# RWKV chunk solve: the second merge level computed on its 64x64 quarter, and independent products moved between the merge steps

## The reference, cut to what matters

```python
def step(S, inp):
    r_t, w_t, k_t, v_t, a_t, b_t = inp
    sa = jnp.einsum('bhvk,bhk->bhv', S, a_t)
    S = (S * w_t[:, :, None, :] + sa[..., None] * b_t[:, :, None, :]
         + v_t[..., None] * k_t[:, :, None, :])
    return S, jnp.einsum('bhvk,bhk->bhv', S, r_t)
```

## Time and profile before

| | us |
|---|---|
| median of 3 runs (lowest to highest) | 2050.32 (2049.99 to 2055.86) |
| the profiled execution: its own time | 2051.84 |
| the profiled execution: span | 2049.4 |
| TensorE busy in the span | 1933.6 |
| VectorE / ScalarE / GpSimd busy | 1138.7 / 761.1 / 693.6 |

### The profile page before, as it was taken

How to read it: one execution, slowest core, us unless ns; L and a number is a source line. 1 busy time by engine, 2 the same in 40 slices (tenths; PEclk the granted TensorE clock), 3 DMA queues, 4 the chain that set the end, 5 groups by cost and what they waited for, 6 DMA issues and landing times. The chain is left out here.

```text
span 2049.4 us, 26280 instructions
## 1 busy us (share of the span) xinstructions
PE 1933.6 (94%) x10768; PEld 1565.2 (76%) x10768; DVE 1138.7 (56%) x1425; ACT 761.1 (37%) x1121; POOL 693.6 (34%) x391
## 2 busy tenths in 40 slices
PE   8998999999999899999999999989989898999994
PEld 6777889998888777788998888869868784555552
DVE  5258755556765427766555676442135335666664
ACT  3345210333222343511132322343346645555552
POOL 0458210324444246821142444434410012333330
PEclk8999999999999999999999999989979998999997
DMA  7322300214444332220021554434310067999973
GB/s 312 95 89 75 103 1 1 84 62 154 176 175 154 118 98 84 81 83 1 21 83 62 194 175 156 137 115 159 113 32 2 21 257 275 343 346 357 344 286 132
DMA packets 78143, 284.63 MB, mean 139 GB/s; under 512 B 27284, under 2 KB 27412, under 8 KB 60741
## 3 DMA queue, kind: packets, MB, share of 16 engines
q1 hardware_dynamic: 71140, 272.36, 38.0%
q0 software_dynamic: 6144, 8.40, 1.2%
q10 hardware_dynamic: 736, 2.14, 0.3%
HBM read 274.44 MB, written 23.63 MB: 145 GB/s over the span
## 5 line engine op out<-in xcount | busy, mean ns | idle before, releaser
L1474 POOL TENSOR_TENSOR wmem_r<-wmem,wmem_r 128x1024 fp32r<-128x1024 f32 x170 | 420.4, 2474 | 665.7 <-ACT wmem_r L998 654.7
L681 PE MATMUL banks<-h_hi_r,wmem_r 128*128 128x512 f32 x1632 | 512.8, 394 | 13.5 <-POOL wmem_r L1474 7.7
L681 PEld LDWEIGHTS banks<-h_hi_r,wmem_r 128*128 128x128 f32 x1632 | 309.0, 189 | 82.0 <-POOL wmem_r L1474 9.5
L998 ACT ACTIVATE wmem_r<-wmem 128x1024 fp32r<-128x1024 f32 x170 | 180.2, 1060 | 484.7 <-DMA wmem<-wstream 481.7
L681 PE MATMUL banks<-hT_r,wmem_r 128*128 128x512 f32 x816 | 319.7, 392 | 0.0
L681 PEld LDWEIGHTS banks<-hT_r,wmem_r 128*128 128x128 f32 x816 | 154.7, 190 | 32.4 <-issue 0.5
L2042 PE MATMUL banks<-wmem_r,gm_mem_r 128*80 128x512 f32 x496 | 178.2, 420 | 0.0
L2570 POOL TENSOR_TENSOR wmem_r<-wmem,wmem_r 128x1024 fp32r<-128x1024 f32 x30 | 74.8, 2492 | 235.4 <-ACT wmem_r L2110 235.4
L1714 POOL DMA_INDIRECT y_tok_dram<-ztp,y_idx x32 | 66.4, 2075 | 221.3 <-DVE ztp L2496 214.8
L702 PE MATMUL banks<-wmem_r,h_hi_r 128*128 128x256 f32 x768 | 140.4, 285 | 0.0
L1414 DVE SCALAR_TENSOR_TENSOR ztp<-xT,c_act,ztp 128x256 f32<-128x256 f32 x168 | 126.6, 754 | 6.0
(11 more groups left out here) (422 smaller groups left out, 3358.0 us busy)
## 6 DMA issues: line engine op xcount, KB each, us to landing
wmem<-wstream SPq DMA_DIRECT2D x206, 512.0 KB, 3.6
slots<-experts SPq DMA_DIRECT2D x80, 1024.0 KB, 6.6
xT<-ada SPq DMA_DIRECT2D x24, 1024.0 KB, 5.8
xT<-experts SPq DMA_DIRECT2D x16, 1024.0 KB
slots<-ada SPq DMA_DIRECT2D x8, 1024.0 KB, 17.8
x_keep<-xT SPq DMA_DIRECT2D x2, 2048.0 KB, 17.6
xT<-x_keep SPq DMA_DIRECT2D x2, 2048.0 KB, 9.2
dil_rows<-dil_once SPq DMA_DIRECT2D x1, 2560.0 KB
```

The costliest lines, as they stand in the source:

```text
L681: mm = nc.tensor.matmul(o, r(lhs[:, k, :]), r(rhs[:, k, :]), start=(k == 0 and i == 0), stop=(k == KD - 1 and i == 2))
L998: inc(nc.scalar.activation(r(chunk(b)[0]), w, ACT.Copy), "w_high")
L1474: inc(g.tensor_tensor(r(lo), lo, r(hi), ALU.subtract), "w_split")
```

## The change

It has three parts. (1) At the second level the mask leaves one 64x64 quarter, so p is computed on it alone: contracted rows 0 to 63, weight columns 64 to 127, moving columns 0 to 63, output partitions 64 to 127. VectorE copies it (no mask) into the unused quarter of `tt`, called `corner`. zn is then another 64x64x64 product, rows 64 to 127 to output partitions 0 to 63, added to the quarter of Z. Four heads of a group now fill 256 columns of a bank on 64 partitions. (2) Products that need no merge result are issued elsewhere on TensorE: w's state products between the two p groups of level 1, w's value products after them, y's state products between p and zn of level 2, y's value products after zn. The u products wait for Z in two groups. (3) The job list follows the new order of opening banks, and since w and y are opened earlier than they are full, the counts that drains wait for come from a table FULL. The mask constant has 128 columns in place of 256.

The core of the diff (the rest passes FULL[name] where JOB[name] + 1 stood, and cuts the constant):

```diff
             for l in range(NL):
                 for g in range(2):
+                    if (l, g) == (0, 1):
+                        job(f"w{n}", "w_ready", 1 + n)
                     job(f"p{n}{l}{g}", "p_ready", 1 + 2 * NL * n + 2 * l + g)
+                if l == NL - 1:
+                    job(f"y{n}", "y_ready", 1 + n)
                 for g in range(2):
...
-            job(f"w{n}", "w_ready", 1 + n)
             job(f"u{n}", "u_ready", 1 + n)
-            job(f"y{n}", "y_ready", 1 + n)
...
+        FULL = {name: j + 1 for name, j in JOB.items()}
+        for n in range(NT):
+            for late, sooner in ((f"w{n}", (f"p{n}01",)), (f"y{n}", (f"zn{n}{NL - 1}0", f"zn{n}{NL - 1}1", f"u{n}"))):
+                FULL[late] += len(sooner)
+                for name in sooner:
+                    FULL[name] -= 1
...
+                def state_part(o, z):
+
+                    for c in range(CW):
+                        nc.tensor.matmul(o[:, c * P:c * P + P], z[:, c, t0:t0 + P], state[:, c, :],
+                                         start=(c == 0), stop=False, skip_group_check=True)
+
+                def value_part(o, k, last):
+
+                    for h in range(RW_H):
+                        cols = slice(h * 64, h * 64 + 64)
+                        mm = nc.tensor.matmul(o[:, cols], gm[:, h, k, :], v_tok[:, n, cols],
+                                              start=(n == 0 and h == 0), stop=(last and h == RW_H - 1), skip_group_check=True)
+                    return mm
+
+                for g in range(2):
+                    if g == 1:
+                        o_w = open_bank(f"w{n}")
+                        if n > 0:
+                            after("s_ready", n)
+                            state_part(o_w, KK)
+                    after("gram_ready", 8 * n + 4 * g + 4)
+                    after("tinit_ready", 2 * n + 1 + g)
+                    o = open_bank(f"p{n}0{g}")
+                    for i in range(4):
+                        u = 4 * g + i
+                        mm = nc.tensor.matmul(o[:, i * P:i * P + P], gm[:, u, 0, :], tt[:, u, :], start=True, stop=True)
+                    full(mm)
                 if n == 0:
                     after("tok_ready")
...
+                full(value_part(o_w, 2, True))
...
+                for g in range(2):
+                    after("t_ready", 2 * (NL - 1) * n + 1 + g)
+                    o = open_bank(f"p{n}1{g}")
+                    for i in range(4):
+                        u = 4 * g + i
+                        mm = nc.tensor.matmul(o[LOWER, i * HALF:i * HALF + HALF], gm[UPPER, u, 0, LOWER], tt[UPPER, u, UPPER],
+                                              start=True, stop=True)
+                    full(mm)
+                o_y = open_bank(f"y{n}")
                 if n > 0:
...
+                    state_part(o_y, R_)
+                for g in range(2):
+                    after("p_ready", 2 * NL * n + 3 + g)
+                    after("z_ready", 2 * NL * n + 1 + g)
+                    o = open_bank(f"zn{n}1{g}")
+                    for i in range(4):
+                        u = 4 * g + i
+                        mm = nc.tensor.matmul(o[UPPER, i * HALF:i * HALF + HALF], corner[LOWER, u, UPPER], zt[LOWER, u, LOWER],
+                                              start=True, stop=True)
+                    full(mm)
+                value_part(o_y, 3, False)
+
+                o_u = open_bank(f"u{n}")
+                after("w_ready", n + 1)
                 for h in range(RW_H):
...
+                    if h % 4 == 0:
+                        after("z_ready", 2 * NL * n + 3 + h // 4)
                     mm = nc.tensor.matmul(o_u[:, h * 64:h * 64 + 64], zt[:, h, :], w_sb[:, h * 64:h * 64 + 64],
                                           start=True, stop=True)
```

And on VectorE:

```diff
+                mask = con("lvl").unsqueeze(1).broadcast_to([P, 4, P])
+                quarter = lambda o, rows: o[rows, 0:4 * HALF].rearrange("p (u t) -> p u t", u=4)
                 for l in range(NL):
...
+                        if l == 0:
+                            inc(v.tensor_tensor(flat(pt, g), o.rearrange("p (u t) -> p u t", u=4), mask, ALU.mult), "p_ready")
+                        else:
+                            inc(v.tensor_copy(flat(corner[LOWER], g)[:, :, UPPER], quarter(o, LOWER)), "p_ready")
...
+                            z_corner = flat(zt[UPPER], g)[:, :, LOWER]
+                            inc(v.tensor_tensor(z_corner, quarter(o, UPPER), z_corner, ALU.add), "z_ready")
```

More of the change, by code:

```diff
@@ L85 @@
     NGLOB += _w
-_names = [("mean", P), ("ones", P), ("freq", 64), ("eps", 1), ("eps_sq", 1), ("ident", P), ("blk64", P), ("gram", W), ("lvl", NL * P),
+_names = [("mean", P), ("ones", P), ("freq", 64), ("eps", 1), ("eps_sq", 1), ("ident", P), ("blk64", P), ("gram", W), ("lvl", P),
           ("ret_mask", W), ("ret_q", W), ("ret_k", 4), ("inv_count", 64), ("off", 2), ("causal", P),
@@ L112, in constants @@
     put("gram", np.concatenate([strict, incl, strict, incl], 1))
-    put("lvl", np.concatenate([((row // b) % 2 == 1) & (col // b == row // b - 1) for b in LEVELS], 1))
+    put("lvl", ((row // SUB) % 2 == 1) & (col // SUB == row // SUB - 1))
     log_gamma = np.log1p(-(2.0 ** (-5.0 - np.arange(RET_H))))
@@ L254, in program @@
         zt, tt, pt = ztp[:, 0], ztp[:, 1], ztp[:, 2]
+        corner = tt
+        HALF = P // 2
+        UPPER, LOWER = slice(0, HALF), slice(HALF, P)
         flat_x2 = X2.rearrange("p c t -> p (c t)")
@@ L378, in program @@
         JOB = {name: j for j, (name, _, _) in enumerate(jobs)}
-        full_of = lambda name: ("bank_full", JOB[name] + 1)
+        FULL = {name: j + 1 for name, j in JOB.items()}
[4 more added lines that the diff above has]
+                    FULL[name] -= 1
+        full_of = lambda name: ("bank_full", FULL[name])
         chunk_used = [full_of(f"r{c}") for c in range(CW)] + [full_of("wl")]
@@ L800, in layer_tensor @@
                     transposes(f"ti{n}{g}", [zt[:, u, :] for u in range(4 * g, 4 * g + 4)])
[L801 to L830, removed]
@@ L844, in layer_tensor @@
[L844 to L854, removed]
@@ L855, in layer_tensor @@
-                after("w_ready", n + 1)
-                after("z_ready", 2 * NL * (n + 1))
-                for h in range(RW_H):
+                full(value_part(o_w, 2, True))
+                for g in range(2):
+                    after("p_ready", 2 * NL * n + 1 + g)
+                    o = open_bank(f"tn{n}0{g}")
+                    for i in range(4):
+                        u = 4 * g + i
+                        mm = nc.tensor.matmul(o[:, i * P:i * P + P], zt[:, u, :], pt[:, u, :], start=True, stop=True)
+                    full(mm)
+                    o = open_bank(f"zn{n}0{g}")
+                    for i in range(4):
+                        u = 4 * g + i
+                        mm = nc.tensor.matmul(o[:, i * P:i * P + P], pt[:, u, :], zt[:, u, :], start=True, stop=True)
+                    full(mm)
@@ L982, in bank @@
             def bank(name):
-                after("bank_full", JOB[name] + 1)
+                after("bank_full", FULL[name])
                 return banks[:, (L * NJ + JOB[name]) % 8]
@@ L1296, in layer_vector @@
                             inc(v.tensor_tensor(flat(tt, g), o, flat(tt, g), ALU.add), "t_ready")
-                        o = bank(f"zn{n}{l}{g}").rearrange("p (u t) -> p u t", u=4)
+                        o = bank(f"zn{n}{l}{g}")
                         if l == 0:
@@ L1509, in layer_gpsimd @@
                 if n > 0:
-                    after("bank_full", JOB[f"u{n - 1}"] + 1)
+                    after("bank_full", FULL[f"u{n - 1}"])
                 inc(g.memset(zt, 0.0), "z_clear")
```

16 lines of the change are left out of this document (4 added, 12 removed).

## The result

| | before | after |
|---|---|---|
| median (lowest to highest) | 2050.15 (2049.69 to 2055.86), 4 runs | 2030.58 (2026.41 to 2035.46), 4 runs |
| ratio, 95% interval | | 0.9893 (0.9868 to 0.9918) |
| profiled execution / span | 2051.84 / 2049.4 | 2035.46 / 2033.0 |
| eight stretches of the solve, one for each chunk | 220.4 | 202.2 |

The kernel became 1.1% faster, 19.6 us by the medians. The forecast of 2034.8 lies 4.2 us above the median and inside what single executions do: the changed kernel's four spread over 9 us.

A forecast was written before the change was run, and what follows sets the result against it. TensorE was taken as the bound, busy 1933.6 of 2049.4 us. Terms 14.5 - 3.4 + 5.4 - 1.0 gave 15.5 us off the profiled 2051.8, so 2036.3, or 2034.8 as a median; range 2028 to 2044.

The forecast's parts named there:

- (a): Second level of the solve: 32 smaller records at 60 ns, 1.92 us in place of 3.73 a chunk; 14.5 us gained.
- (b): TensorE's switches between whole array and quarter: 28 edges at 0.12 us each, 3.4 us lost.
- (c): w's state products, 0.89 us, fit the 1.50 us hole between first-level groups in six later chunks; 5.4 us gained.
- (d): Moved products cover waits for VectorE in the second level; only first chunks wait, 0.5 us before z, 1.0 us lost.
- Rival 1: Second level: the quarter's records keep the pace of 112 ns, so 2.0 us is gained, 2048.3 us; chance 0.08.
- Rival 2: TensorE drains at each edge, costing 0.36 us in place of 0.12; gain 8.8 us, 2041.5 us; chance 0.10.
- (e): y's reused bank and the counts: nothing waits, nothing put on it; at most 0.6 us a chunk if late.
- (f): Clock in the solve: the smaller hole may spare a 1.6 us stretch, quarter products may bring others; only in the range.
- rival 3: Quarter products halve the clock in the solve, 1.6 us a stretch; two per chunk give 2060.4 us; chance 0.05.
- Rival 4: Something after the solve sets the pace, so the solve's gain does not reach the end: 2050.3 us; chance 0.03.

The follow-up runs named there:

- the two form kernels: The changed kernel with second-level products loading 128 weight columns (2053.29 us), or contracting all 128 rows with 64 weight columns (2029.56 us), one execution each.
- the repeat: The changed kernel run again with no edit: 2032.59 us, ratio 0.9897.
- the later split: The kernel before, with GpSimd's split of the next weight block held back until the second level's masks: 2042.0 us, ratio 0.9943.
- the order alone: The kernel before with only w's and y's state and value products moved, both levels keeping full 128x128 products: 2047.42 us, ratio 0.997.

## Why the prediction was right

**The sum.** 15.5 us was forecast in the solve and 15.1 measured at full clock; 2034.8 was forecast and 2030.6 measured. The direction and the place held, and the terms by what they measured: (a) 15.0 for 14.5, (b) 4.6 lost for 3.4, (c) 5.3 for 5.4, (d) 0.8 lost for 1.0, and 0.3 won by moved products in the first chunks, which the sum did not have. That makes 15.2. The solve's total is closer than (b) alone would have left it, because its error and those of the others cancel in part; that is luck in the size, not in the mechanism.

**(a) The quarter's pace.** The line through 80 and 128 weight columns gave 60 ns, and 58 was measured: (3.73 - 32 x 0.058) x 8 = 15.0. That it is the weight columns, not rows, is shown by the two form kernels. Rival 1 (112 ns) fell.

**(b) The edges.** This is the term most off. It took 0.12 us an edge from the Gram stage; adding two edges cost 0.33, 0.17 each. The term was 28 x 0.12 = 3.4 and is about 28 x 0.165 = 4.6. Rival 2 (0.36 each, a full drain) fell. The Trainium skill (TensorEngine Tiling (Array Packing), "Key Properties") says that a change of tiling mode drains TensorE. The trace agrees in that each change costs something, about half of the 0.36; whether that is a drain, no run shows.

**(c) The hole.** 0.89 us filled, as forecast, and the hole's end did not move. What the text said of its cause was incomplete: it put the hole down to masks that begin after the state update, and did not see that 2 us of that update was waiting for GpSimd. That did not touch this sum, but it hid a cheap change that fills the same hole: had the decays' minimum and maximum been asked for by line, 339 against 2507 ns would have shown it.

**(d) The cover.** Right in kind and somewhat too large. A first chunk's wait before z cost 0.38 us for 0.5, inside the stated bounds, and u without cover waits 0.2 for 0.6, which is in no term of the sum. What was mis-sized is the price of VectorE's operations on 64x256 elements, taken like those on 128x512 (0.44 us at most, not 0.69), and, for u, the count from z's last record though u starts with the first group.

**(e) Banks.** Nothing waited for y's bank: a Gram stage takes 4.96 us for 4.97 before.

**(f) and rival 3.** The clock was not lost in every chunk, but it did fall in the solve in one of two profiles of the changed kernel (7.0 us in layer 0) and in three chunks with wide weights. Over all executions (4, and 5 of the repeat) the changed kernel stays between 2026.41 and 2036.78 us, below every one of the kernel before (2044.76 at the least), so such a stretch did not eat the gain. Of the ten profiles with 64x64 or 128x64 products in the level, only that of the repeat lost more than 2 us in a chunk. Three without them (the kernel before, its version with the later split, the order alone) lost at most 1.6. That is too few to say whether the quarter makes long stretches more frequent.

**Rival 4.** It fell, since the solve's gain arrived: 15.1 us there, 19.6 in the medians, 20.3 in the repeat. Where the other 4 to 5 us come from is open. The part outside the solve took between 1824 and 1835 us in the profiles, and the clock in the solve another few, so medians of few executions can differ by that much; that the forecast missed them by 4.2 says nothing against its terms.

## What to carry to other kernels

The small fp32 products here are priced by their weight columns (58 ns a record at 64, 112 at 128), so halve those first, and group products of one form, since each change of form cost 0.17 us. Before filling a hole with moved work, ask by line for the minimum and maximum of each instruction that stands ahead of it. If one lasts many times its minimum and ends just after another engine's instruction does, it may be waiting for that one; moving the other instruction tests it, and may close the hole with no other change. A wait is measured from start to start, since the idle time that the profile prints starts only at the end of the last record.

## What the hardware showed that was not expected

A VectorE operation on two SBUF operands that started after a GpSimd operation of two SBUF operands stood until that one had ended: up to 2507 ns for 341. A 64-column weight load with all 128 rows costs nearly the same as with 64 rows (138 and 135 ns). And the granted clock fell to half behind the second level of the first chunk in both layers when the weights were 128 columns wide on 64 rows, and stayed there for 8 us and more with TensorE busy throughout (919.00 to 927.00: 0.50, busy 8.00 of 8.00). The same happened in layer 0 of the changed kernel's repeat, with 64-column weights, and not in its first profile; no run here tells why.
